# Spreading root columns over the partitions: product with the identity or transposition

## The reference

```python
def rms_norm_f32(t, gain):
    t32 = t.astype(jnp.float32)
    return t32 * lax.rsqrt(jnp.mean(t32 * t32, axis=-1, keepdims=True) + EPS) * gain.astype(jnp.float32)

# first block: layer 0 retention (4 heads), layer 1 chunked attention (16 heads)
h = (rms_norm_f32(x, norm_g[i]) * (1.0 + scale) + shift).astype(x.dtype)
x = x + (gate * mixer(h)).astype(x.dtype)
# second block
h = rms_norm(x, norm_mix)                 # gated delta rule, sparse attention (top-k), convolution
x = x + jnp.concatenate([y_a, y_b, y_c], axis=-1) @ w_out
x = x + memory_cross_attention(rms_norm(x, norm_cross), rms_norm(mem, norm_mem), ...)
x = x + jnp.square(jax.nn.relu(rms_norm(x, norm_mlp) @ mlp_w1)) @ mlp_w2
```

## Time and profile before

| | before |
|---|---|
| median of 3 runs | 1919.26 us (1912.92 to 1921.46) |
| span of the profiled execution | 1914.3 us |
| TensorE busy | 1854.2 us, 97% |
| weight loads busy | 1532.8 us, 80% |
| GpSimd busy | 1105.3 us, 58% |
| VectorE busy | 852.5 us, 45% |
| ScalarE busy | 461.7 us, 24% |

### The profile page before, as it was taken

How to read it: one execution, slowest core, us unless ns; L and a number is a source line. 1 busy time by engine, 2 the same in 40 slices (tenths; PEclk the granted TensorE clock), 3 DMA queues, 4 the chain that set the end, 5 groups by cost and what they waited for, 6 DMA issues and landing times.

```text
span 1914.3 us, 26822 instructions
## 1 busy us (share of the span) xinstructions
PE 1854.2 (97%) x9638; PEld 1532.8 (80%) x9638; DVE 852.5 (45%) x1433; ACT 461.7 (24%) x938; POOL 1105.3 (58%) x848
## 2 busy tenths in 40 slices
PE   8999999999999999999999999989899899999997
PEld 4888888888888888888878778877878688878886
DVE  5733516165334323343242696886363563213311
ACT  3120211110222222221221236555231422002200
POOL 2746546489354444554446658964067298667862
PEclk9999999999899999999999999999999999999999
DMA  9423222275232223322223332200033133332331
GB/s 352 140 69 99 68 80 71 77 270 175 66 88 77 75 66 87 87 76 71 60 82 90 93 87 52 60 23 23 1 99 89 41 107 97 100 96 81 99 95 44
DMA packets 279473, 172.81 MB, mean 90 GB/s; under 512 B 5937, under 2 KB 269937, under 8 KB 278385
## 3 DMA queue, kind: packets, MB, share of 16 engines
q1 hardware_dynamic: 272912, 151.01, 27.1%
q10 hardware_dynamic: 6496, 20.93, 3.3%
HBM read 169.69 MB, written 2.10 MB: 90 GB/s over the span
## 4 chain that ended last, share of the span: by engine, by line
PE 87%; DVE 8%; ACT 2%; DMA 1%; issue 1%; POOL 1%; SPq 0%; ACTq 0%; POOLq 0%; DVEq 0%
PE acc L380 16%; PE acc L382 16%; PE acc L381 16%; PE acc L428 3%; PE acc L429 3%; PE acc L430 3%; PE st L441 3%; PE acc L410 3%; PE acc L411 2%; PE acc L412 2%; DVE conv_out L2431 2%; PE sc L1495 2%; PE ob L1414 2%; PE sc L1475 2%; PE bc L474 1%; PE sc L1377 1%
## 5 line engine op out<-in xcount | busy, mean ns | idle before, releaser
L739 POOL TENSOR_TENSOR wl<-raw,wh 128x512 fp32r<-128x512 f32 x456 | 647.0, 1440 | 19.4
L736 POOL TENSOR_SCALAR wh<-raw 128x1024 fp32r<-128x1024 f32 (+1 forms) x232 | 261.7, 1128 | 664.4 <-PE acc L382 255.5
L380 PE MATMUL acc<-hh,wh 128*128 128x512 f32 x800 | 324.3, 405 | 0.3 <-ACT sq L1346 0.3
L382 PE MATMUL acc<-hh,wl 128*128 128x512 f32 x800 | 313.7, 392 | 0.0
L381 PE MATMUL acc<-hl,wh 128*128 128x512 f32 x800 | 312.8, 391 | 0.0
L380 PE MATMUL acc<-Yh,wh 128*128 128x512 f32 x512 | 203.6, 398 | 0.0
L381 PE MATMUL acc<-Yl,wh 128*128 128x512 f32 x512 | 202.4, 395 | 0.0
L382 PE MATMUL acc<-Yh,wl 128*128 128x512 f32 x512 | 202.3, 395 | 0.0
L380 PEld LDWEIGHTS acc<-hh,wh 128*128 128x128 f32 x800 | 151.1, 189 | 34.5 <-issue 2.9
L381 PEld LDWEIGHTS acc<-hl,wh 128*128 128x128 f32 x800 | 151.1, 189 | 32.4 <-issue 2.4
L382 PEld LDWEIGHTS acc<-hh,wl 128*128 128x128 f32 x800 | 150.7, 188 | 32.3
(11 more groups left out here) (450 smaller groups left out, 3086.1 us busy)
## 6 DMA issues: line engine op xcount, KB each, us to landing
raw<-in_att_w_in SPq DMA_DIRECT2D x64, 512.0 KB, 4.1
raw<-in_mlp_w SPq DMA_DIRECT2D x64, 512.0 KB, 4.0
raw<-in_ret_w_in SPq DMA_DIRECT2D x48, 512.0 KB, 3.8
ada_w<-in_ada_w ACTq DMA_DIRECT2D x8, 1536.0 KB, 7.3
raw<-in_w_in SPq DMA_DIRECT2D x23, 512.0 KB, 3.8
ada_w<-in_ada_w SPq DMA_DIRECT2D x16, 512.0 KB, 10.4
raw<-in_ret_w_out SPq DMA_DIRECT2D x16, 512.0 KB, 4.3
raw<-in_att_w_out SPq DMA_DIRECT2D x16, 512.0 KB, 4.1
```

Source lines behind the costliest of these rows:

```text
L380: e.matmul(bank[:, :], wh[:, s, k, :], rhs_high(k), start=(start and k == 0), stop=False)
L382: last = e.matmul(bank[:, :], wl[:, s, k, :], rhs_high(k), start=False, stop=(stop and k == k1 - 1))
L736: e.tensor_scalar(wh[:, s, 0:k1, :], raw[:, s, 0:k1, :], 1.0, 1.0, ALU.mult, ALU.mult).then_inc(high_done, 1)
L739: low = e.tensor_tensor(wl[:, s, k0:k0 + KT // 2, :], raw[:, s, k0:k0 + KT // 2, :], wh[:, s, k0:k0 + KT // 2, :].bitcast(F32), ALU.subtract)
```

## The change

In `spread` and in the DSA key rows the product of the repeated column with the identity becomes a transposition of the repeated column, an instruction that is given the identity too. Every value out[j, m] is column[m] in both.

```diff
         def spread(e, name, n=NT, c0=0, bank=None):
 
             for t in range(n):
-                last = e.matmul((bc if bank is None else bank)[:, t * P:(t + 1) * P],
-                                rs[:, 0, c0 + t:c0 + t + 1].to_broadcast([P, P]), ident, start=True, stop=True)
+                last = e.transpose((bc if bank is None else bank)[:, t * P:(t + 1) * P],
+                                   rs[:, 0, c0 + t:c0 + t + 1].to_broadcast([P, P]), ident)
             last.then_inc(*PE.done(name))
...
                 for t in range(NT):
-                    last = e.matmul(bc[:, t * P:(t + 1) * P], dkc[:, t:t + 1].to_broadcast([P, P]), ident,
-                                    start=True, stop=True)
+                    last = e.transpose(bc[:, t * P:(t + 1) * P], dkc[:, t:t + 1].to_broadcast([P, P]), ident)
                 last.then_inc(*PE.done("d_bc"))
```

## The result

| | before | after |
|---|---|---|
| median of 4 runs, us | 1916.8 (1912.9 to 1921.5) | 1900.8 (1896.0 to 1903.0) |
| ratio, run against run | | 0.9899 (0.988 to 0.9917) |
| span of the profiled execution, us | 1914.3 | 1897.7 |
| its mean granted clock of TensorE | 0.987 | 0.989 |
| TensorE busy, us | 1854.2 | 1836.5 |

Another run of the kernel before had come in by then, which took its median from 1919.3 to 1916.8. The change makes the kernel faster by 0.8 to 1.2%, and the time lies in the range that was given.

A forecast was written before the change was run, and what follows sets the result against it. TensorE, busy for 97% of the span, was taken to bound the kernel. Gains of 12.7 + 0.22 + 0.96 + 1.05 = 14.9 us, taken from 1919.3, gave 1904.4 us; range 1898 to 1910.

The forecast's parts named there:

- What one record holds up: On TensorE, 0.11 us a record; a spread of four calls goes from 0.89 to 0.44 us, 0.45 less.
- The bound of 0.09 us: Lower bound for one transposition on TensorE, from the shorter spacing of the rows; a gain of 0.53 us a group.
- Which groups count: Spreads on the chain: 28 groups at full clock for 12.7 us, nk 0.22, n1 0.96, GDN output 1.05.
- the GDN output: Four groups at 1379 and 1384: 0.6 us for the first two, limited by VectorE, 0.45 for the last two; 1.05.
- The n1 spread: At 483 us, 1.93 us long at the lower clock with VectorE waiting for it; half, 0.96 us, goes.
- passed on in full: Mixer stage, VectorE's top-k at 1252: its 3.03 us wait for TensorE lets the three earlier spreads' 1.4 us reach the time.
- From the span to the time: Whole kernel: the median of the runs stands 5.0 us above the profiled span, taken as the same after.
- the rise and fall of the clock: Rival around n1 and the GDN output: transpositions keep the clock low or let it fall, costing 4 us; 1908, chance 0.03.
- The wait for att_v: Rival in attention: TensorE waits for ScalarE's copy behind the spread, losing 3.6 us of gain in 8 places; 1908, chance 0.06.
- The two records: Rival in the spreads: a transposition of a repeated column is issued as two records, so nothing changes; 1919, chance 0.04.
- the load that can't overlap: Rival in the spreads: the transposing load can't run under the product before, a group takes 1.10 us; 1926, chance 0.03.
- a saving larger than half: Rival in the spreads: a transposition holds up a quarter of the product, 0.22 us a group; 1897, chance 0.02.

The follow-up runs named there:

- e8: Kernel after, with attention's sums of squares made as fp32r products, one record each; median 1884.1 us, ratio 0.9814 to before.
- e4: Kernel before, with all calls outside attention made transpositions and attention's spreads left as products; median 1909.8 us, ratio 0.9951 to before.
- e1: Kernel before, run again without an edit; median 1920.9 us, ratio 1.0001 to before.
- e5: Kernel after, with the transpositions of each spread issued twice, 130 calls more; median 1918.0 us, ratio 0.9997 to before.
- e6: Kernel before, with the products of each spread issued twice, 130 calls more; median 1945.8 us, ratio 1.0149 to before.
- e7: Kernel after, with attention's 16 spreads as single fp32r products instead of transpositions; median 1893.9 us, ratio 0.9875 to before.
- e9: Kernel after, with an unused tile of 32 bytes in each partition ahead of the region holding Yh and Yl; median 1896.9 us, ratio 0.9878 to before.
- e11: e8 with retention's sums of squares made in fp32r as well; median 1875.6 us, ratio 0.9781 to before.

## Why the prediction was right or wrong

*What one record holds up.* Right. 0.36 and 0.44 us from start to start, 0.45 less in the chain, 0.105 and 0.216 us a call when the calls are doubled. The bound of 0.09 us was not reached by the chain, and repetition of the column costs nothing. The Trainium skill's page "FP8 and Floating Point Precision" (TensorE Precision Notes) has true FP32 at four passes through the array. Four times 128 columns at 2.4 GHz are 0.213 us, and 0.216 was measured; but that is no test of it, since the fp32 sums of squares, which stream a single column, cost 0.79/4 = 0.20 us a call too (e8). The factor of 4 for the transpose mode in FP32 that the Trainium skill's page "TensorE: Matmul & The Clock Gate" (Terms) has is not borne out: the runs show 28.1/13.7 = 2.05.

*Which groups count.* Right for attention (7.5 us measured, 16 x 0.45 = 7.2) and for the rest in sum. Two of its terms were a little off, and cancel in part. For the GDN output I had 1.05; from the start of its first spread to the product that waits for VectorE, it is 1388.96 - 1378.86 = 10.10 us before and 8.72 after, so 1.4. The first pair did not lose 0.3 to VectorE. The n1 spread took 1.13 in the chain for 1.93, a gain of 0.80 where I had 0.96, as it began its weight load behind a wait for the roots (0.8 us, L469). Before, TensorE was itself late there: the clock had fallen earlier, at 479 us, and the sixteen small products of L1462 ahead of the spread took 3.6 us, where after they took 1.9. VectorE's wait at the top-k shrank and stayed:

```profile
1238.98 2.16 DVE L2524 SCALAR_TENSOR_TENSOR gdn_qk_t<-ob,gdn_cols,gdn_g 128x128 f32<-128x128 f32 x8 [2.05 <-PE ob L1715]
```

2.05 us for the 3.03 of the earlier trace rows: the gain was passed on to this point, where VectorE is 12.99 us ahead of the kernel before. That it was passed on in full does not hold to the end of the stage: at the first spread of the GDN output TensorE is 12.38 us ahead (1378.86 less 1366.48). Where the 0.6 us went is open; VectorE's lead has fallen to 12.4 by 1321 us of the trace before.

*The sum.* 14.9 us, measured 15.1 to 15.8 at an equal clock.

*From the span to the time.* This is the step that failed. I took the 5.0 us between the median and the profiled span as the same after. An execution's time lies only 1.8 us above its own span (1899.5 and 1897.7 for the one profiled after, and 1.7 to 1.9 in all others but six of e4, with 2.0 to 3.3); the other 3.2 were the distance between one execution and the median of three. That this is the clock is likely and not shown for those three, whose clocks are not on record: in e1's runs the same spread goes with it. From the four runs' median, 1916.8 - 14.9 = 1901.9, and 1900.8 was measured; 2.5 of the 3.6 us by which the forecast was high are thus the median of before, which a fourth run moved. For the same reason the trace's difference, 16.6 us, is larger than the sum: more time at the lower level in the execution before than in the one after (52 and 44 us), mean clock 0.987 and 0.989, which at 1.6 us for 0.001 are 3.2 us. That would leave 13.4 for the spreads, 1.5 under the sum, which single executions can't settle. I counted the rise and fall of the clock as a rival only in the way of a cost, and had no term for it as chance of either sign.

*The rivals.* The wait for att_v can be read off directly: no idle time stands before the record behind the spread at 579.48, and the copy ends at 579.92, well after it.

```profile
579.32 0.60 ACT L969 ACTIVATE att_v<-acc 128x512 f32<-128x512 f32 x1 [8.35 <-PE sc L1495]
```

The nearness in the earlier trace rows was chance. The clock did not fall through transpositions: the stretch of the earlier trace rows, with 4 more transpositions in it, kept 1.00, and so did attention from 505 to 960 us, with 64 transpositions of repeated columns and 140 of L1487.

```profile
505.00:960.00 455.00, 455.00 (x2556) 386.72 (x2556) 170.00 (x349) 115.39 (x282) 223.09 (x187) 1.00 0.29 80
535.00:582.00 47.00, 47.00 (x265) 39.87 (x264) 18.57 (x39) 14.31 (x36) 20.14 (x17) 1.00 0.33 89
```

The Trainium skill's sentence that the full clock doesn't engage for the transpose mode ("TensorE: Matmul & The Clock Gate", Part 4) is not borne out among products; no run here has transpositions alone. The two records are ruled out by the 134 records, the load that can't overlap and a saving larger than half by e5 and e6.

## What to carry to other kernels

Price a small matrix instruction by the distance between starts in a dense stretch, not by its duration, and count its records: where a weight load of 128 columns comes with each, a record of 128 columns or fewer costs 0.085 to 0.11 us here, so such an fp32 product that a transposition or an fp32r product can replace gives back half, 0.1 us a call, for as long as TensorE is never idle. Before comparing two kernels within 1%, set their executions to the same mean granted clock, or what you measure is which of them was granted more. And after adding or removing a small tile, look at where the large ones start and at the distance of the products that stream them: a shift of 32 bytes was worth more than a third of this change, and would have been put down to the edit of e7 or e8.

## What the runs showed of the hardware that was not expected

Some of the places at the lower clock level differ between executions of the same kernel, though TensorE waits at the same places each time; the mean granted clock went from 0.980 to 0.991 and accounts for nearly all of the scatter, 1.6 us for each 0.001. Products with the 128x512 fp32r moving operands Yh and Yl in the region at 109728 or 109792 stand 233.3 ns apart in the mean; with the region at 109760 or 110272 they stand 228.9 apart, but for one stretch of 82 us in e8, at 233.4; those on hh, at a multiple of 64 all along, 227 to 228. Only two starts at a multiple of 64 (one of them shared by e8, e9 and e11) and two at 32 more than one were tried, and neither why the start matters nor what switched the distance in e8 was looked into. The weight load of a column repeated over 128 by a step of 0 took 139 ns in transposing form, no more than that of an ordinary tile (L1487 149, L1985 140).
